# The three gate products of each recurrent block, moved one piece later on TensorE

## The chip, the cores and the metric

The kernel runs on one core of one Trainium2 chip. The metric is the device time of one launch in microseconds (us); lower is better. The five engines of the core run apart from each other and meet only in semaphores: TensorE (PE in the rows; its weight loads are PEld), VectorE (DVE), ScalarE (ACT), GpSimd (POOL) and SyncE (SP), which starts transfers.

## What is computed

One inference step of a hybrid decoder layer on 1024 prompt tokens and 8 sample tokens (1032 columns in all) with a model width of 1024. It has a recurrent branch (RG-LRU), a dilated attention branch, a merge of the two and a SwiGLU FFN. Only the recurrent branch matters here. Cut to its core:

```python
xn = rmsnorm(x, norm_mix)
lru_x, lru_g, q, k, v = split(xn @ w_in)
xc = causal_conv(lru_x, w_conv, b_conv)            # four taps
gate_a = einsum('btni,nij->btnj', xc, w_a) + b_a   # 16 blocks of 64 x 64
gate_x = einsum('btni,nij->btnj', xc, w_x) + b_x
r, i = sigmoid(gate_a), sigmoid(gate_x)
log_a = -8 * r * softplus(-lam)
a, mult = exp(log_a), sqrt(-expm1(2 * log_a))
u = mult * i * xc
h_t = a_t * h_{t-1} + u_t                          # a scan over the tokens
y_lru = (h * gelu(lru_g)) @ w_branch_lru
```

## The kernel before

The width is cut into eight blocks of 128 channels; channels lie on partitions, tokens along the free axis. A block of the recurrent stage needs two projections of the normed input, each called a **unit**: slot 0 gives the convolution's input `lru_x`, slot 1 gives `lru_g`. A unit is 72 matmuls (8 tiles of the contraction times 3 products of a split float32), in three **pieces** of 24, one for each third of the columns (344), and lands in its slot of the PSUM tile `ups`. The next stage, "qk", has units of the same size; its first one, qk(0, slot 0), follows the last recurrent block.

Between the pieces stand the **gate products**: `gates(i, c)` multiplies block i's convolved tile `XC` with the two 128 x 128 gate matrices in `bd`, for third c of the columns, into the two banks of `aux`. In a trace one call is four matmuls and four weight loads of line L754. All three calls of a block use the same two banks, so each waits in line L752 (`gate_ev`) until ScalarE has read the one before; the first also waits in L750 and L751 for the gate matrices and for the whole convolution (`xc_done`).

Here is one block on the other engines. The order is written out by hand and each engine keeps to it:

- VectorE: `side_in(i-1)` (L1571) takes slot 1 out of PSUM and frees it (`ps_free[1]`); `gated(i-1)` (L1578) multiplies the gate I with XC and waits for all three gates of block i-1; `branch_in(i)` (L1565) takes slot 0 out of PSUM; `conv(i)` (L1583, L1586) makes XC; `recur(i-1)` (L1594, L1595, L1599, the scan L1600, L1604) is the recurrence.
- ScalarE: `gate(i-1, 1)` (L1151, L1152: two sigmoids), GELU (L1158, behind `side_in`), `gate(i-1, 2)`, the transfers of the next gate matrices, `front(i)` (L1145, L1146), exp and tanh, the root L1169 in the midst of `recur(i-1)`, then `gate(i, 0)`. L1151 and L1158 need different function tables, each loaded in turn.
- GpSimd: `split` (L564, then L566) of the next weights, each time PE has finished a unit.

`front(i)` overwrites XC, so it waits for `gated(i-1)`; this ties one block of the recurrence to the next. In the qk stage PE's `stats` calls (L809) wait for GpSimd's low part of a square (L591, L596), which comes from a tile that VectorE takes out of PSUM at L1631. The first such tile comes before `recur(7)` in VectorE's order, the second after it.

Of the kernel before, what the change touches and what calls it, by code (L numbers as in the profile page):

```python
# [33 lines left out]
NCH = 3  # L34
CH = NT // NCH
KT = D // P
# [59 lines left out]
def build(nc, A, O):  # L96

    with ExitStack() as ctx:
        def sb(name, shape, dt=F32):
            return ctx.enter_context(nc.sbuf_tensor(name, shape, dt))  # L100
# [10 lines left out]
        big1 = sb("big1", [P, 2, KT, NT], F32R)  # L111
# [40 lines left out]
        def tmp(n):  # L152

            return x1[:, n, :]
# [557 lines left out]
        def _(pe):  # L712
            def unit(name, i, slot, src, nk=KT, parts=(0, 1, 2), ready=None, hi=0, held=None):

                if 0 in parts:
                    pe.wait_ge(w_split[slot], i + (T0[name] + 2))
                    if not held:
                        pe.wait_ge(ps_free[slot], i + (T0[name] + 1 - (12 if T0[name] >= T0["ylru"] else 0)))
                for c in parts:
                    if held:  # L720
                        held(c)
                    for k in range(nk):
                        if ready:
                            ready(c, k)
                        for n, (w, a) in enumerate(((0, hi), (0, 1 - hi), (1, hi))):
                            ins = nc.tensor.matmul(ups[:, slot, c, 0:CH], wsp[:, slot, w, k, :], src[:, a, k, c * CH:(c + 1) * CH],  # L726
                                                   start=(k == 0 and n == 0), stop=(k == nk - 1 and n == 2))
                if NCH - 1 in parts:
                    ins.then_inc(unit_done[slot], 1)
# [18 lines left out]
            def gates(i, c):  # L748
                if c == 0:
                    pe.wait_ge(bd_loaded, i * 64 + 64)  # L750
                    pe.wait_ge(xc_done, i + 1)  # L751
                pe.wait_ge(gate_ev, i * NCH + (c + 1))  # L752
                for a in range(2):
                    ins = nc.tensor.matmul(aux[:, a, 0:CH], bd[:, a, :], tmp(0)[:, c * CH:(c + 1) * CH], start=True, stop=True)  # L754
                ins.then_inc(gate_mm, 1)
# [18 lines left out]
            def lru(i):  # L774
                for c in range(NCH):
                    unit("lru", i, 0, big1, parts=(c,))
                    if c < 2:
                        gates(i - 1, c + 1)
                unit("lru", i, 1, big1)
                gates(i, 0)  # L780

            def first_evacuated(c):

# [2 lines left out]
            by_tiles("lru", big1, x_split)  # L786
            unit("lru", 0, 1, big1, parts=(0, 1))
            unit("lru", 0, 1, big1, parts=(2,), ready=norm_rows)
            unit("lru", 1, 0, big1, parts=(0, 1), held=first_evacuated)
            gates(0, 0)  # L790

            def second_gates(c, k):
                if k == 4:
                    gates(0, 1)

            unit("lru", 1, 0, big1, parts=(2,), held=first_evacuated, ready=second_gates)
            gates(0, 2)
            unit("lru", 1, 1, big1)
            gates(1, 0)
            with pe.Fori(2, KT) as i:  # L800
                lru(i)

            def stats(j, i, low=sq_parts[1]):

                pe.wait_ge(qsl_done[j], i + 1)
                pe.wait_ge(rt_done[1 - j], i + 1)
                for c in range(2):
                    for a, part_of in enumerate((sq_parts[0], low)):
                        ins = nc.tensor.matmul(aux[:, c, :], bones_r[:], part_of[:, c * 512:(c + 1) * 512], start=(a == 0), stop=(a == 1))  # L809
                ins.then_inc(st_done[j], 1)  # L810

            def qk(i, first):
                for j in range(2):
                    if first and j == 0:
                        for c in range(NCH):
                            unit("qk", i, j, big1, parts=(c,))
                            if c < 2:
                                gates(KT - 1, c + 1)
                    else:
                        unit("qk", i, j, big1)  # L820
                    if j:
                        if first:
                            pe.wait_ge(gate_ev, KT * NCH + 1)
                            stats(0, 0, first_low)
                        else:
                            stats(0, i)
                    elif not first:
                        stats(1, i - 1)

            pe.sem_inc(rt_done[1], 1)  # L830
            pe.sem_inc(st_done[1], 1)
            qk(0, True)
            with pe.Fori(1, 12) as i:
                qk(i, False)
# [25 lines left out]
            for g in range(NG):  # L860
                with pe.Fori(0, 4) as i:
# [20 lines left out]
                    for n in range(10):  # L882
# [19 lines left out]
                        if n >= 2:  # L902
# [4 lines left out]
                            for hh in range(2):  # L907
                                for k in range(nk):
                                    c = 256 * hh + 256 - P * (nk - k)
# [1236 lines left out]
```

## Time and profile before

| | us |
|---|---|
| median of three runs (lowest, highest) | 1946.58 (1945.2, 1947.05) |
| the profiled execution | 1945.86 |
| its span, first to last instruction | 1944.1 |
| mean granted TensorE clock | 0.998 of full speed |

The recurrent stage stands from about 40 to 245 us of the span, followed by the qk stage. The profiled execution is 0.72 us under the median and has 1.76 us around its span. Starts and durations in the rows are those of this execution.

### The profile page before, as it was taken

To read this page: it belongs to the slowest core of one execution; us is meant where nothing else is said; L and a number is where in the kernel's file an instruction comes from. 1 tells how busy PE (TensorE), PEld (TensorE's weight loads), DVE (VectorE), ACT (ScalarE), POOL (GpSimd) and SP (SyncE) were. 2 spreads that over 40 slices of the span, in tenths; PEclk is the share of its full clock that TensorE was granted. 3 is DMA by queue.
4 is the path that set the end of the run, shared out by engine and by line. 5 is a ranking of instruction groups with operands and counts; after the bars stand their busy time and mean duration, and the time that the engine had idled before them with its cause. 6 is when DMAs were issued, how large, how long until landed. Compare 5 with 4: busy or idle time off the path is not lost.

```text
span 1944.1 us, 34565 instructions
## 1 busy us (share of the span) xinstructions
PE 1918.2 (99%) x13148; PEld 1870.2 (96%) x13148; DVE 1145.4 (59%) x1373; ACT 616.8 (32%) x1035; POOL 873.3 (45%) x533
## 2 busy tenths in 40 slices
PE   7999999999999999999999999999999999999999
PEld 7899999999999999999999999999999999999999
DVE  5666688878844545444328663586554555455555
ACT  5655632222203333333320111333222232223222
POOL 3233254444434433534334332336655656455643
PEclk9999999999999999999999999999999999999999
DMA  6111112222254355544345652112111111211112
GB/s 244 43 46 35 45 70 86 86 86 86 87 171 131 128 158 173 171 160 149 128 161 182 209 194 87 65 33 66 50 39 50 61 55 34 65 45 61 34 59 110
DMA packets 85034, 191.73 MB, mean 99 GB/s; under 512 B 10445, under 2 KB 38600, under 8 KB 83408
## 3 DMA queue, kind: packets, MB, share of 16 engines
q1 hardware_dynamic: 57872, 142.92, 22.3%
q10 hardware_dynamic: 27072, 47.53, 7.1%
q8 instruction: 65, 1.06, 0.2%
q14 instruction: 25, 0.20, 0.0%
HBM read 147.81 MB, written 42.62 MB: 98 GB/s over the span
## 4 chain that ended last, share of the span: by engine, by line
PE 88%; DVE 5%; issue 2%; DMA 1%; ACT 1%; POOL 1%; ACTq 1%; SPq 0%; DVEq 0%; POOLq 0%
PE ups L726 30%; PE ups L870 14%; PE ups L995 13%; PE ups L1038 11%; PE aux L1038 8%; PE aux L910 3%; PE ups L889 2%; PE aux L900 1%; PE ups L767 1%; PE aux L809 1%; DVE x L1583 1%; DMA big_f<-x_R 1%; PE aux L754 1%; PE ups L900 1%; ACTq L1090 1%
## 5 line engine op out<-in xcount | busy, mean ns | idle before, releaser
L726 PE MATMUL ups<-big,wsp 128*128 128x344 f32 x4680 | 755.1, 321 | 0.7 <-issue 0.7
L726 PEld LDWEIGHTS ups<-big,wsp 128*128 128x128 f32 x4680 | 739.9, 188 | 8.8 <-issue 1.6
L564 POOL CAST wsp<-wraw 128x1024 fp32r<-128x1024 f32 (+1 forms) x96 | 104.6, 1089 | 658.0 <-issue 393.9
L674 POOL TENSOR_TENSOR wsp<-wraw,wsp 128x512 fp32r<-128x512 f32 x184 | 263.7, 1449 | 212.4 <-ACT wsp L1406 212.4
L870 PE MATMUL ups<-big,wsp 128*128 128x344 f32 x1728 | 302.6, 326 | 0.0
L870 PEld LDWEIGHTS ups<-big,wsp 128*128 128x128 f32 x1728 | 271.4, 189 | 3.5 <-issue 3.0
L995 PE MATMUL ups<-big,wsp 128*128 128x344 f32 x1584 | 254.4, 320 | 0.3 <-DVEq L1979 0.2
L995 PEld LDWEIGHTS ups<-big,wsp 128*128 128x128 f32 x1584 | 248.9, 188 | 3.9 <-issue 2.9
L1038 PE MATMUL ups<-big,wsp 128*128 128x258 f32 x1920 | 240.7, 283 | 1.4 <-ACT ext L1445 1.3
L1038 PEld LDWEIGHTS ups<-big,wsp 128*128 128x128 f32 x1920 | 234.9, 189 | 1.8 <-issue 1.8
L566 POOL TENSOR_TENSOR wsp<-wraw,wsp 128x1024 fp32r<-128x1024 f32 (+1 forms) x96 | 228.7, 2382 | 7.7
L1406 ACT ACTIVATE wsp<-wraw 128x512 fp32r<-128x512 f32 x184 | 113.2, 626 | 257.1 <-PE ups L995 128.7
L1038 PE MATMUL aux<-big,wsp 128*128 128x258 f32 x1440 | 181.5, 282 | 0.0
L1038 PEld LDWEIGHTS aux<-big,wsp 128*128 128x128 f32 x1440 | 175.9, 189 | 0.0
L2001 DVE TENSOR_TENSOR x<-ups,x 128x1032 f32<-128x1032 f32 x87 | 107.2, 1232 | 116.1 <-PE ups L995 116.1
L1645 DVE RECIPROCAL x<-x 128x1024 f32<-128x1024 f32 x24 | 157.2, 6551 | 5.0 <-ACT x L1222 4.9
L683 POOL TENSOR_TENSOR wraw<-wraw 128x512 f32<-128x512 f32 x80 | 112.3, 1404 | 71.1 <-DMA wraw<-w_ffn_in 63.1
L1785 DVE SCALAR_TENSOR_TENSOR x<-ups,ext 128x256 f32<-128x256 f32 (+1 forms) x96 | 52.0, 542 | 134.5 <-PE ups L889 133.8
L1222 ACT ACTIVATE x<-aux,epst 128x1024 f32<-128x1024 f32 x24 | 26.8, 1117 | 204.4 <-PE aux L809 194.1
L1302 ACT ACTIVATE x<-x 128x128 f32<-128x128 f32 (+1 forms) x192 | 75.5, 442 | 11.6 <-DVE x L1788 11.6
L910 PE MATMUL aux<-ext,x 128*128 128x65 f32 x560 | 73.1, 266 | 0.0
L1792 DVE COPY x<-aux 128x130 f32<-128x130 f32 x96 | 28.0, 292 | 74.6 <-PE aux L910 73.4
(248 smaller groups left out, 1870.5 us busy)
## 6 DMA issues: line engine op xcount, KB each, us to landing
wraw<-w_in SPq DMA_DIRECT2D x52, 512.0 KB, 3.9
wraw<-w_ffn_in SPq DMA_DIRECT2D x80, 256.0 KB, 2.6
x<-out_qkv SPq DMA_DIRECT2D x35, 512.0 KB, 4.2
out_qkv<-x ACTq DMA_DIRECT2D x32, 512.0 KB, 3.3
wraw<-w_ffn_out SPq DMA_DIRECT2D x44, 256.0 KB, 2.8
x<-gate_s SPq DMA_DIRECT2D x16, 516.0 KB, 4.6
wraw<-w_merge SPq DMA_DIRECT2D x16, 512.0 KB, 6.7
x<-o_s SPq DMA_DIRECT2D x8, 792.0 KB, 4.8
```

The costliest lines, as they stand in the source:

```text
L564: nc.gpsimd.tensor_copy(hi, raw).then_inc(w_hi, 1)
L566: nc.gpsimd.tensor_tensor(lo, raw, hi.bitcast(F32), ALU.subtract).then_inc(w_split[slot], 1)
L674: nc.gpsimd.tensor_tensor(lo, raw_at(b), hi.bitcast(F32), ALU.subtract).then_inc(f_lo, 1)
L683: nc.gpsimd.tensor_tensor(raw(to), raw(a), raw(b), op).then_inc(f_add, 1)
L726: ins = nc.tensor.matmul(ups[:, slot, c, 0:CH], wsp[:, slot, w, k, :], src[:, a, k, c * CH:(c + 1) * CH], start=(k == 0 and n == 0), stop= ...
L870: ins = nc.tensor.matmul(ups[:, 0, c, 0:CH], wsp[:, slot, w, k, :], big1[:, a2, k, c * CH:(c + 1) * CH], start=(k == 0 and w + a2 == 0), s ...
L910: ins = nc.tensor.matmul(o_bank[:, hh * (HD + 1):(hh + 1) * (HD + 1)], PTS[q % 2][:, c:c + P], VTOK[:, q + 1 - nk + k, hh, :], start=(k == ...
L995: ins = nc.tensor.matmul(ups[:, n % 2, c, 0:CH], w[:, n % 2 * 2 + k, :], part(hid_row(a, k), c), start=(k == 0 and m == 0), stop=(k == 1 a ...
L1038: ins = nc.tensor.matmul(bank[s], w[:, kk, :], sub(MOVING[n](a, kk), s), start=(first and kk == 0 and m == 0), stop=(kk == 3 and m == 2), ...
L1406: nc.scalar.activation(ring(b)[0], raw_at(b), ACT.Copy).then_inc(f_hi, 1)
L1645: step.step(nc.vector.reciprocal(rms_t, rms_t))
L2001: nc.vector.tensor_tensor(own, ups_v[n % 2], own, ALU.add).then_inc(d_ev, 1)
```

## The change

Each gate product stands one piece later on PE. In the loop, `gates(i, 0)` stood after the last piece of unit (i, slot 1), and `gates(i, 1)` and `gates(i, 2)` after the first and second piece of unit (i+1, slot 0). Now the three calls stand after the first, second and third piece of unit (i+1, slot 0). For block 0 they stand after the last piece of unit (1, slot 0) and the first two of (1, slot 1); for block 7 behind the three pieces of qk(0, slot 0). Nothing is added or taken away and no other engine's order changes.

```diff
             def lru(i):
                 for c in range(NCH):
                     unit("lru", i, 0, big1, parts=(c,))
-                    if c < 2:
-                        gates(i - 1, c + 1)
+                    gates(i - 1, c)
                 unit("lru", i, 1, big1)
-                gates(i, 0)
...
-            unit("lru", 1, 0, big1, parts=(0, 1), held=first_evacuated)
-            gates(0, 0)
-
-            def second_gates(c, k):
-                if k == 4:
-                    gates(0, 1)
-
-            unit("lru", 1, 0, big1, parts=(2,), held=first_evacuated, ready=second_gates)
-            gates(0, 2)
-            unit("lru", 1, 1, big1)
-            gates(1, 0)
+            unit("lru", 1, 0, big1, held=first_evacuated)
+            for c in range(NCH):
+                gates(0, c)
+                unit("lru", 1, 1, big1, parts=(c,))
...
-                            if c < 2:
-                                gates(KT - 1, c + 1)
+                            gates(KT - 1, c)
```

PE at the entry of the stage, from the second piece of unit (1, slot 0) to the head of the loop. The rows name the semaphores each instruction waits for:

```order
 L726 MATMUL ups<-big,wsp 128x344 x23
+L726 MATMUL ups<-big,wsp 128x344 [waits lx_done]
+L726 MATMUL ups<-big,wsp 128x344 x23
 L754 MATMUL aux<-x,bd 128x344 [waits gate_ev,xc_done,bd_loaded]
 L754 MATMUL aux<-x,bd 128x344
-L726 MATMUL ups<-big,wsp 128x344 [waits lx_done]
-L726 MATMUL ups<-big,wsp 128x344 x11
+L726 MATMUL ups<-big,wsp 128x344 [waits ps_free1,w_split1]
+L726 MATMUL ups<-big,wsp 128x344 x23
 L754 MATMUL aux<-x,bd 128x344 [waits gate_ev]
 L754 MATMUL aux<-x,bd 128x344
```

The first gate product of block 0 has moved from behind the second piece to behind the third, and the second one now has a whole piece of slot 1 ahead of it where it had half a piece of slot 0.

PE in the loop, from the third piece of unit (i, slot 0) to the loop's end:

```order
 L726 MATMUL ups<-big,wsp 128x344 x24
-L726 MATMUL ups<-big,wsp 128x344 [waits ps_free1,w_split1]
-L726 MATMUL ups<-big,wsp 128x344 x71
-L750 ISA
-L752 ISA [waits xc_done,bd_loaded]
+L752 REGISTER_ALU
 L754 MATMUL aux<-x,bd 128x344 [waits gate_ev]
 L754 MATMUL aux<-x,bd 128x344
-L800 REGISTER_ALU
-L800 COMPARE_AND_BRANCH
+L726 MATMUL ups<-big,wsp 128x344 [waits ps_free1,w_split1]
+L726 MATMUL ups<-big,wsp 128x344 x71
```

The 72 matmuls of slot 1 stood between the end of slot 0 and a gate product of the same block; now a gate product of block i-1, the third, stands ahead of them.

## Rows read from the trace of the kernel before

**Rows 1.** The page: busy time of each engine, share of the span, instructions.

```profile
PE 1918.2 (99%) x13148; PEld 1870.2 (96%) x13148; DVE 1145.4 (59%) x1373; ACT 616.8 (32%) x1035; POOL 873.3 (45%) x533
```

**Rows 2.** Waits on PE: who waited for whom, us in total, times, longest.

```profile
PE aux L754 <- ACT x L1152: 3.0, 3, 1.3
```

**Rows 3.** Timeline of PE: start, duration, line, tiles, [idle before and releaser].

```profile
50.05 1.39 PE L754 MATMUL aux<-x,bd 128*128 128x344 f32 x4 [0.42 <-issue]
...
53.89 1.42 PE L754 MATMUL aux<-x,bd 128*128 128x344 f32 x4 [0.56 <-ACT x L1152]
...
75.98 1.42 PE L754 MATMUL aux<-x,bd 128*128 128x344 f32 x4 [1.33 <-ACT x L1152]
76.98 4.20 PE L726 MATMUL ups<-big,wsp 128*128 128x344 f32 x24
...
134.17 15.53 PE L726 MATMUL ups<-big,wsp 128*128 128x344 f32 x96
149.53 1.32 PE L754 MATMUL aux<-x,bd 128*128 128x344 f32 x4
150.43 4.20 PE L726 MATMUL ups<-big,wsp 128*128 128x344 f32 x24
154.46 1.32 PE L754 MATMUL aux<-x,bd 128*128 128x344 f32 x4
...
208.03 1.42 PE L754 MATMUL aux<-x,bd 128*128 128x344 f32 x4 [1.15 <-ACT x L1152]
...
268.13 1.20 PE L809 MATMUL aux<-ext_r,bones_r 128*128 128x512 f32 x4 [0.27 <-POOL ext_r L596]
```

**Rows 4.** Timeline of DVE, same columns.

```profile
61.56 1.23 DVE L1578 TENSOR_TENSOR ext<-x 128x1032 f32<-128x1032 f32 x1 [3.08 <-ACT x L1152]
64.61 3.93 DVE L1583 SCALAR_TENSOR_TENSOR x<-ext,par,x 128x1024 f32<-128x1024 f32 x3 [1.82 <-ACT x L1146]
68.57 0.75 DVE L1586 SCALAR_TENSOR_TENSOR x<-stc,par,x 128x8 f32<-128x8 f32 x3
...
86.24 1.23 DVE L1565 TENSOR_TENSOR ext<-ups,ext 128x1032 f32<-128x1032 f32 x1
...
133.49 1.23 DVE L1571 TENSOR_TENSOR x<-ups,ext 128x1032 f32<-128x1032 f32 x1 [0.69 <-DVEq L1605]
138.14 1.24 DVE L1578 TENSOR_TENSOR ext<-x 128x1032 f32<-128x1032 f32 x1 [3.42 <-ACT x L1152]
139.29 1.23 DVE L1565 TENSOR_TENSOR ext<-ups,ext 128x1032 f32<-128x1032 f32 x1
...
151.63 3.17 DVE L1599 TENSOR_TENSOR x<-x,ext 128x1032 f32<-128x1032 f32 x1
...
245.26 1.23 DVE L1631 TENSOR_TENSOR x<-ups,ext 128x1032 f32<-128x1032 f32 x1
...
261.51 1.23 DVE L1631 TENSOR_TENSOR x<-ups,ext 128x1032 f32<-128x1032 f32 x1 [0.36 <-DVEq L1606]
```

**Rows 5.** Timeline of ACT, same columns.

```profile
51.56 1.28 ACT L1151 ACT_TABLE_LOAD   x1 [8.37 <-PE aux L754]
...
53.30 0.54 ACT L1152 ACTIVATE x<-aux,par 128x344 f32<-128x344 f32 x1
...
58.17 1.07 ACT L1158 ACTIVATE x<-x 128x1032 f32<-128x1032 f32 x1
...
150.36 1.07 ACT L1169 ACTIVATE x<-x 128x1032 f32<-128x1032 f32 x1 [2.85 <-DVE x L1595]
...
153.19 0.54 ACT L1152 ACTIVATE x<-aux,par 128x344 f32<-128x344 f32 x1
```

**Rows 6.** Timeline of POOL, same columns.

```profile
69.87 1.57 POOL L564 CAST wsp<-wraw 128x1024 fp32r<-128x1024 f32 x1 [8.97 <-issue]
...
149.86 1.38 POOL L564 CAST wsp<-wraw 128x1024 fp32r<-128x1024 f32 x1 [7.11 <-issue]
151.31 2.40 POOL L566 TENSOR_TENSOR wsp<-wraw,wsp 128x1024 fp32r<-128x1024 f32 x1
```

## The prediction

> **What bounds the kernel now.** First the page's busy times: PE is busy 99% of the span and every other engine 59% or less [rows 1]. The table of waits says that PE's gate products waited for ScalarE's sigmoids 3.0 us in three places [rows 2]. PE's timeline has the places: 0.56 us at 53.89, 1.33 at 75.98, 1.15 at 208.03, and 0.42 at 50.05, where block 0's convolution had just ended [rows 3]. That is 3.46 us, the most that moving these products can give back.
>
> Next, what PE needs for a block without waits. A gate call takes 0.90 us until the next matmul (149.53 to 150.43), a piece 4.03 us until the gate call behind it (150.43 to 154.46), and 96 matmuls 15.36 us (134.17 to 149.53) [rows 3]. A block is 3 x 0.90 + 2 x 4.03 + 15.36 = 26.12 us, before and after: the change has the same pieces and seams.
>
> Then the others, on which this case hangs. VectorE takes slot 0 of block 2 out of PSUM at 86.24 and the first qk tile at 245.26 [rows 4]: 159.02 us for six blocks, 26.50 each. That is more than PE's 26.12. VectorE and ScalarE form a **chain** that runs by itself: `side_in`, GELU, the third gate, `gated`, `branch_in`, `front`, `conv`, `recur`, and `side_in` again. It is less than 60% busy on each engine because they take turns, but it has no slack as a whole. In block 4 the third gate's sigmoids wait for GELU, and `gated` waits 3.42 us for them (138.14) [rows 4]; PE had written that product at 133.3. So PE is fed by the chain, and PE's waits at 75.98 and 208.03 are places where the chain has come too late.
>
> At the stage's end the chain decides too. The second qk tile leaves PSUM at 261.51, behind the last recurrence [rows 4], and PE's `stats` at 268.13 waits 0.27 us for what GpSimd makes of it [rows 3]. There is no slack there: what the chain loses by then, PE waits.
>
> **Term 1, the entry: +5.7 us.** Block 0's first product was reached at 49.63 (50.05 less 0.42) [rows 3]. It now has a piece ahead of it: 49.63 + 4.03 = 53.65. The second follows at 53.65 + 0.90 + 4.03 = 58.6, the third at 63.5. From the start of a product to the end of its sigmoids, with a table load between, it is 3.79 us (50.05 to 53.30 + 0.54) [rows 3, 5]. GELU's input is long there (GELU ran at 58.17) [rows 5]; it would run at 62.5, between the second and third gate, and be done before the third product is. So the third gate ends at 67.3 and `gated(0)` starts there, not at 61.56 [rows 4]: +5.7. Everything up to `branch_in(2)` hangs on it, since `front(1)` overwrites what `gated(0)` reads. PE does not need to wait yet: the sigmoids of the first product end at 57.4, ahead of 58.6.
>
> **Term 2, block 1: +0.6 us.** `conv(1)` starts 3.05 us after `gated(0)` (61.56 to 64.61) [rows 4], at 70.35. GpSimd's split starts when PE ends unit (1, slot 1), now about 68.5; before it was 69.87 [rows 6]. Two SBUF operands on VectorE and a GpSimd instruction exclude each other here: L1599 takes 3.17 us at 151.63, where GpSimd's subtraction runs until 153.71, and ends 1.09 us behind it [rows 4, 6]. Without a GpSimd instruction such a tile takes 1.23 (L1578) [rows 4]. The split holds 1.04 + 0.08 + 2.40 us, to 72.0, so `conv(1)` loses 1.65 us. It ended 7.76 us after `gated(0)` (68.57 + 0.75) [rows 4] and now ends at 67.3 + 7.76 + 1.65 = 76.7. PE reaches gates(1, 0) at 72.3: **a new wait of about 4.4 us**, longer than all the waits that go. The second product of block 1 then waits some 0.9 us more for its sigmoids, and the third stands at 87.6. Its sigmoids end at 91.4, and `branch_in(2)` follows 1.15 us behind `gated(1)`, as at 138.14 and 139.29 [rows 4]: 92.55 against 86.24. That is +6.3, of which 5.7 is term 1.
>
> **Term 3, six blocks: +1.2 us.** Now the third product stands behind slot 0's last piece, and the cycle runs through PE. Third product to the end of its sigmoids 3.79; to `gated` 0.03; to `branch_in` 1.15; from there to the root L1169 11.07 (139.29 to 150.36) [rows 4, 5]; to the end of the next block's first gate 3.37 (150.36 to 153.73) [rows 5]; to the second product 0.05; to the third 1.00 + 4.03 (the 1.00 from 75.98 to 76.98) [rows 3]. Sum 24.5 us. To this comes the collision with the split of slot 1. That split starts 12.7 us behind the third product (0.90 + 11.33 + 0.5) and holds the pair until 16.2 or later; L1594 and L1595 stand at 13.5 and 14.8, so they lose about 2.2 us; L1599, which lost 1.94 in the block at 151.63, then comes after it. 24.5 + 2.2 = 26.7 a block against 26.50 now: six blocks, +1.2. The ends: with no collision PE's 26.12 is the floor, 6 x (26.12 - 26.50) = -2.3; with GpSimd's copy in a convolution step and its subtraction in L1594 it is 1.2 us worse a block, +7. I take the middle since the starts put it there. With 26.7, PE waits some 0.5 us for L1152 at each second gate product, and slot 1 of PSUM is free 0.8 us before PE wants it.
>
> **Term 4, the exit: -0.4 us.** From 245.26 to 261.51 it is 16.25 us [rows 4], which holds several instructions that GpSimd held up. Placed again from 252.75, GpSimd's low part of the first tile, the last root and the split behind `stats` fall so that the second tile leaves at about 268.6: 15.85 us. It can be 2 us either way. PE itself would reach the second `stats` at about 272.7, with 1.5 us of new wait at the first one; the chain has it ready at 275.2. So PE waits 2.5 us more, and the stage is left at 275.2, not 268.13.
>
> **Sum.** 5.7 + 0.6 + 1.2 - 0.4 = **+7.1 us**. The qk stage behind it moves with PE as a whole. From the profiled execution's 1945.86 that is 1953.0; from the median, 0.72 us higher, **1953.7**. PE's four old waits are not a further term: PE no longer decides when the stage ends.
>
> The page "Perfetto Trace Analysis" of the Trainium skill, sections "Identifying the Most-Contended Engine" and "Optimization Strategy", says to take the engine with the highest occupancy, find the gaps between its slices and make what they depend on come sooner. By it the three waits on ScalarE are what the move is worth, and the sum would be a gain; what the chain of two half-busy engines costs would not be in it. It is the first rival.
>
> **Rivals.** (a) *Faster*: PE decides throughout, the four waits go and the chain's lag stays hidden. 1946.58 - 3.46 = **1943.1**. For it: the share of 99% [rows 1], and that each second product gets 4.9 us more time behind L1169. Against it: the wait at 268.13 shows no slack at the exit, and the 11.07 us from `branch_in` to the root [rows 4, 5]. It decides if the lag at block 1 is under the 3.8 us or so that the new place gives gates(1, 0); I get more than 7. (b) *The chain catches up*: no collision in the loop (-2.3 for +1.2) and an exit 2.5 us better than 16.25. 6.3 - 2.3 - 2.5 = +1.5: **1948.1**. For it: PE's floor is under the chain's 26.50, and the collisions depend on tenths of a microsecond. Against it: a split of 3.5 us comes twice a block, with VectorE at work two thirds of the time. (c) *Two collisions a block*: +7 for the +1.2 in term 3: +12.9, **1959.5**. For it: GpSimd's subtraction for slot 0 ends within 0.1 us of `gated`'s start, and the copy for slot 1 starts as the convolution ends. Against it: a hold at `gated` would last only its last tenths.
>
> **How the numbers follow.** Forecast 0.66, (a) 0.11, (b) 0.15, (c) 0.08. A measurement of this kernel can tell about 0.2%, 3.9 us, from no change. The forecast's own range goes from +4.5 to +9.5, by the exit's 2 us and the cycle: 1951 to 1956. The range takes in (b) and part of (c): 1948.0 to 1957.5. (a) falls just inside 0.2%, except where a little more is won: faster 0.04. Within 0.2%: the rest of (a), most of (b) and the low edge of the forecast, 0.23. Slower 0.73.
>
> **What would show it.** In the changed kernel's trace: `gated(0)` near 67.3; PE idle about 4.4 us before the gate product near 76.7, released by L1586; `branch_in(2)` near 92.5; loop blocks of about 26.7 us with L1595 or L1594 long and L1599 at 1.23; idle before the second `stats` of 2 to 3 us, released by L596. The forecast is wrong if PE reaches gates(1, 0) without a wait, if blocks fall to 26.12, or if the `stats` wait is gone.

## The result

| | us, median (lowest, highest) | profiled execution | span |
|---|---|---|---|
| before, 6 runs | 1946.8 (1945.13, 1947.13) | 1945.86 | 1944.1 |
| changed, 6 runs | 1957.94 (1956.94, 1963.18) | 1957.09 | 1955.2 |

The change makes the kernel slower: ratio 1.0064, 95% interval 1.0052 to 1.0076, about 11 us. The forecast was +7.1 us (1953.7) with a range up to 1957.5. The direction held; the forecast size was two thirds of what came, and the time lies just above the range.

PE's waits in the changed kernel (who waited for whom, us in total, times, longest):

```profile
PE aux L754 <- DVE x L1576: 4.7, 1, 4.7
PE aux L754 <- ACT x L1142: 3.1, 6, 0.7
...
PE aux L800 <- POOL ext_r L596: 2.2, 1, 2.2
```

Lines behind the edit have moved up by ten in the changed kernel: L1576 is the L1586 of before, L1142 is L1152, and so on; `stats` is L800 instead of L809. Where [rows 2] had 3.0 us, the gate products now wait 4.7 us in one place for the convolution, 0.5 to 0.7 us in each of six blocks for the sigmoids, and the second `stats` waits 2.2 us. The timeline of PE has the places (start, duration, [idle before]); they answer [rows 3]:

```profile
51.65 1.32 PE L754 MATMUL aux<-x,bd 128*128 128x344 f32 x4
...
75.03 2.36 PE L754 MATMUL aux<-x,bd 128*128 128x344 f32 x4 [4.65 <-DVE x L1576]
...
108.89 1.42 PE L754 MATMUL aux<-x,bd 128*128 128x344 f32 x4 [0.50 <-ACT x L1142]
...
277.70 1.20 PE L800 MATMUL aux<-ext_r,bones_r 128*128 128x512 f32 x4 [2.19 <-POOL ext_r L596]
```

And VectorE, to set beside [rows 4]: `gated(0)`, `conv(1)`, `branch_in(2)`, `conv(2)`'s short steps, two instructions of `recur`, and the two qk tiles.

```profile
65.26 1.24 DVE L1568 TENSOR_TENSOR ext<-x 128x1032 f32<-128x1032 f32 x1 [12.18 <-ACT x L1142]
68.31 5.68 DVE L1573 SCALAR_TENSOR_TENSOR x<-ext,par,x 128x1024 f32<-128x1024 f32 x3 [1.82 <-ACT x L1136]
...
91.50 1.23 DVE L1555 TENSOR_TENSOR ext<-ups,ext 128x1032 f32<-128x1032 f32 x1
...
99.12 3.84 DVE L1576 SCALAR_TENSOR_TENSOR x<-stc,par,x 128x8 f32<-128x8 f32 x3 [0.18 <-DVE x L1573]
...
104.21 1.23 DVE L1585 SCALAR_TENSOR_TENSOR x<-x 128x1032 f32<-128x1032 f32 x1
...
106.74 1.24 DVE L1589 TENSOR_TENSOR x<-x,ext 128x1032 f32<-128x1032 f32 x1
...
255.62 1.23 DVE L1621 TENSOR_TENSOR x<-ups,ext 128x1032 f32<-128x1032 f32 x1
...
271.06 1.23 DVE L1621 TENSOR_TENSOR x<-ups,ext 128x1032 f32<-128x1032 f32 x1 [0.36 <-DVEq L1596]
```

From 91.50 to 255.62 are six blocks in 164.12 us, 27.35 each; before they took 26.50. The short steps of the convolution, three of eight columns, take 3.84 us at 99.12, where three such steps took 0.75 at 68.57 in [rows 4] (0.97 in a block of the loop without a split on them, as shown below). L1589, the L1599 of before, is down from 3.17 to 1.24. GpSimd's split stands on the short steps:

```profile
99.43 1.04 POOL L564 CAST wsp<-wraw 128x1024 fp32r<-128x1024 f32 x1 [8.96 <-issue]
100.55 2.39 POOL L566 TENSOR_TENSOR wsp<-wraw,wsp 128x1024 fp32r<-128x1024 f32 x1
```

It does so in every block from 2 to 7 (3.84 to 3.89 us). That is where the prediction's third term went wrong. In the kernel before GpSimd paid a part of the collision (its copy took 1.38 us at 149.86 [rows 6]); here its copy takes 1.04 us, and VectorE pays all of it. So the two engines also hold each other up where no semaphore stands between them, unlike what the opening section says of the five engines.

### The profile page after: what moved, and what is told of

Read it like the earlier page. It is cut to its first block, busy times and chain, and to the rows that moved or that the text cites. A ratio compares the mean times of both kernels' runs of the same rounds, so it can differ in the third digit from the quotient of the medians.

```text
span 1955.2 us, 34565 instructions
## 1 busy us (share of the span) xinstructions
PE 1923.0 (98%) x13148; PEld 1871.1 (96%) x13148; DVE 1154.9 (59%) x1373; ACT 617.5 (32%) x1035; POOL 861.0 (44%) x533
## 4 chain that ended last, share of the span: by engine, by line
PE 87%; DVE 5%; issue 3%; ACT 1%; DMA 1%; POOL 1%; ACTq 1%; SPq 0%; DVEq 0%; POOLq 0%
PE ups L726 30%; PE ups L860 14%; PE ups L985 13%; PE ups L1028 11%; PE aux L1028 8%; PE aux L900 3%; PE ups L879 2%; DVE x L1573 1%; PE aux L754 1%; PE aux L890 1%; PE ups L767 1%; PE aux L800 1%; DMA big_f<-x_R 1%; PE ups L890 1%; ACTq L1080 1%
## 5 line engine op out<-in xcount | busy, mean ns | idle before, releaser
L564 POOL CAST wsp<-wraw 128x1024 fp32r<-128x1024 f32 (+1 forms) x96 | 99.9, 1041 | 672.7 <-issue 403.8
L674 POOL TENSOR_TENSOR wsp<-wraw,wsp 128x512 fp32r<-128x512 f32 x184 | 256.2, 1408 | 214.1 <-ACT wsp L1396 214.0
L1292 ACT ACTIVATE x<-x 128x128 f32<-128x128 f32 (+1 forms) x192 | 75.5, 443 | 10.9 <-DVE x L1778 10.9
```

The lines of the kernel that those rows point to most:

```text
L564: nc.gpsimd.tensor_copy(hi, raw).then_inc(w_hi, 1)
L674: nc.gpsimd.tensor_tensor(lo, raw_at(b), hi.bitcast(F32), ALU.subtract).then_inc(f_lo, 1)
```

## The experiments

The loss can be read off at two places of a trace: the mean block from `branch_in(2)` to the first qk tile, and the start of the second `stats`, where the stage is left. All runs are in one table. The kernel before was timed again on the chip of each group: 1947.14 us for the first four experiments, 1946.9 for the next four, 1946.59 for the last three. The traces do not enter the stage at the same time: PE goes on with its unit at 39.72 us in the trace of before, at 38.32 in the changed kernel's first one, and between 39.06 and 40.07 in the others. So differences of about 1 us between two rows of the last two time columns show nothing by themselves.

| kernel | median us | ratio to before (95%) | branch_in(2) | block, mean of six | second stats |
|---|---|---|---|---|---|
| before | | | 86.24 | 26.50 | 268.13 |
| changed | 1957.94 | 1.0064 (1.0052, 1.0076) | 91.50 | 27.35 | 277.70 |
| entry_only | 1953.74 | 1.0035 (1.0024, 1.0047) | 93.41 | 26.52 | 275.38 |
| loop_only | 1953.7 | 1.0038 (1.0023, 1.0053) | 88.02 | 27.35 | 274.13 |
| after_parked | 1950.1 | 1.0019 (1.0009, 1.0029) | 92.42 | 26.35 | 272.53 |
| exit_undone | 1961.1 | 1.008 (1.0062, 1.0098) | 93.24 | 27.47 | 282.37 |
| before_parked | 1947.2 | 1.0002 (0.9993, 1.0011) | 87.17 | 26.14 | 267.31 |
| loop_parked | 1943.41 | 0.9981 (0.9972, 0.9991) | 87.55 | 26.19 | 264.20 |
| after_swapped | 1960.48 (one run) | | 93.70 | 27.23 | 279.15 |
| after_again | 1958.83 | 1.0062 (1.0045, 1.0078) | 92.86 | 27.35 | 279.12 |
| before_parked_b | 1944.49 | 0.9986 (0.9978, 0.9995) | 85.60 | 26.14 | 265.74 |
| loop_parked_again | 1942.65 | 0.9979 (0.9968, 0.9991) | 88.39 | 26.19 | 265.04 |
| after_parked_b | 1946.16 | 0.9995 (0.9986, 1.0004) | 92.03 | 26.18 | 268.27 |

**The theory**: the chain of VectorE and ScalarE sets the stage, the change delays its start, and the new phase puts GpSimd's split on the chain in each block. **The rivals**: PE's own waits are the loss, or the third product's place behind slot 0 makes a block long whatever GpSimd does.

### Either half of the change alone

entry_only has the new entry, and the loop and the qk stage of before. Against the changed kernel's entry:

```diff
             for c in range(NCH):
                 gates(0, c)
                 unit("lru", 1, 1, big1, parts=(c,))
+            gates(1, 0)
```

> The kernel before with only the entry of the changed one: block 0's three gate products stand behind the last piece of unit (1, slot 0) and the first two of (1, slot 1); the loop and the qk stage are those of before. Chain theory (the lag of VectorE's and ScalarE's chain is what PE pays at the stage's exit): gated(0) starts about 5 us later, gates(1, 0) waits about 8 us for the convolution, blocks of 26.5 us as before, time +5 to +6.5 us over the kernel before, about 1952.5. Rival (the loss is made in the loop, the entry is hidden): within 2 us of the kernel before.

loop_only has the old entry without its last line, and the loop and the qk stage of the changed kernel. Against the entry of before:

```diff
             gates(0, 2)
             unit("lru", 1, 1, big1)
-            gates(1, 0)
```

> The changed kernel with the entry of before: block 0's gate products where they stood, block 1's and all later ones at the new places. Chain theory: branch_in(2) about 2 us later than before, no wait of 4.7 us, but the same phase between GpSimd's splits and the three small convolution steps L1586, so blocks of 27.3 us, +6 to +7 us over the kernel before, about 1953. Rival (the entry's lag is what makes the collision): blocks of 26.5 us or less, +2 us or less.

Both came out by the chain theory: +6.6 us for each by the medians, for entry_only just above the 5 to 6.5 that were expected. entry_only keeps blocks of 26.52 us and carries a lag of 7.2 us from `branch_in(2)` to the exit, unchanged (93.41 against 86.24, 275.38 against 268.13). Its new wait for the convolution (which ends at 76.08) is longer than in the full change, since gates(1, 0) is still at the old place:

```profile
76.18 2.63 PE L754 MATMUL aux<-x,bd 128*128 128x344 f32 x4 [8.22 <-issue]
```

loop_only is only 1.8 us late at `branch_in(2)` and has no such wait, but its blocks take 27.35 us. So the collision does not need the late entry: the loop's phase alone makes it. The two halves are not fully separate: they add up to 13.2 us, more than the 11 of the whole. The 1.8 us come from block 1's products at the new places, and the full change has them too.

### GpSimd's split taken off the chain

In after_parked the weights' split of slot 1 waits for the end of the running recurrence, from block 2 on:

```diff
+                if name == "lru":
+                    split(name, nk, 1, 0)
+                    split(name, nk, 1, 1)
+                    with pool.Fori(2, KT) as i:
+                        split(name, nk, i, 0)
+                        pool.wait_ge(z_done, i)
+                        split(name, nk, i, 1)
+                    continue
```

> The changed kernel, but from block 2 on GpSimd starts the split of slot 1's weights only when the running recurrence is over (it waits for z_done), so that it falls where VectorE waits or reads PSUM. Collision theory: the three small steps take about 1 us together again, blocks fall from 27.33 to PE's floor of 26.1 to 26.2 us, conv(1) takes 3.9 instead of 5.7 us, and the time is 8 to 9 us under the changed kernel, about 1949. Rival (the third gate product behind slot 0's last piece sets the block's length, whatever GpSimd does): blocks stay near 27.3 us and at most the 1.7 us of conv(1) is won, 1956 to 1958. A second risk: the split comes late for unit (i, slot 1), which would show as a PE wait for GpSimd's L566.

By the medians it is 3.0 us over the kernel before instead of 11.1: about 8 us are gone. In the trace the short steps are back at 0.97 us:

```profile
121.87 4.14 DVE L1581 SCALAR_TENSOR_TENSOR x<-ext,par,x 128x1024 f32<-128x1024 f32 x3 [2.02 <-ACT x L1144]
126.19 0.97 DVE L1584 SCALAR_TENSOR_TENSOR x<-stc,par,x 128x8 f32<-128x8 f32 x3 [0.18 <-DVE x L1581]
```

`branch_in` comes every 26.16 us there (118.63 to 223.26, four blocks); the mean of 26.35 in the table includes the last block, where the qk stage's split still collides. The parked splits now reach into `gated` (1.87 us at 116.84 instead of 1.23), but the block no longer hangs on it: it is at PE's 26.1. Nothing on PE was moved, so the rival that the product's place makes the block long falls. `conv(1)` is free of the split too, and PE waits 2.90 us for it instead of 4.65. That wait and the chain's lag at the exit (2.13 us before the second `stats`) are the waits that are left.

### Is it the short steps, or the hold?

after_swapped puts the three short steps of the convolution ahead of its long ones, so that the split meets long instructions:

```diff
                 dve.wait_ge(xc0_done, i + 1)
-                for k in range(1, 4):
-                    step.step(nc.vector.scalar_tensor_tensor(XC[:, 0:SEQ], LX[:, k:k + SEQ], par[:, ds(i, 1), k], XC[:, 0:SEQ], ALU.mult, ALU.add))
                 for k in range(3):
...
+                for k in range(1, 4):
+                    ins = nc.vector.scalar_tensor_tensor(XC[:, 0:SEQ], LX[:, k:k + SEQ], par[:, ds(i, 1), k], XC[:, 0:SEQ], ALU.mult, ALU.add)
+                    if k < 3:
+                        step.step(ins)
                 ins.then_inc(xc_done, 1)
```

> The changed kernel with the three 8-column steps of the convolution ahead of its three 1024-column ones, so that GpSimd's split of slot 1 meets a long step and L1584, L1585 instead of the short ones. If what counts is only how long GpSimd holds VectorE off (about 2.9 us wherever it falls), blocks stay at 27.2 to 27.4 us. If short instructions are what makes it dear, blocks fall to about 26.7 us, the figure of the prediction.

Blocks of 27.23 us, in one run. Now other instructions pay: the plain copy behind the convolution takes 1.01 us where it took 0.16 in the changed kernel, and L1585 3.29 us where it took 1.23.

```profile
129.28 1.01 DVE L1580 COPY sout<-ext 128x11 f32 x1
...
131.46 3.29 DVE L1585 SCALAR_TENSOR_TENSOR x<-x 128x1032 f32<-128x1032 f32 x1
```

The sum is about 2.9 us again. What counts here is how long GpSimd holds VectorE off while VectorE has work, not which instruction is met. The copy has only one SBUF operand, and yet it ended at 130.29, with GpSimd's copy (130.26). So in this trace the exclusion is not limited to instructions with two, as term 2 of the prediction had it.

### The exit

exit_undone is the changed kernel with block 7's products at the places of before:

```diff
                     if first and j == 0:
+                        gates(KT - 1, 0)
                         for c in range(NCH):
                             unit("qk", i, j, big1, parts=(c,))
-                            gates(KT - 1, c)
+                            if c < 2:
+                                gates(KT - 1, c + 1)
```

> The changed kernel with block 7's gate products at the places of before (one ahead of qk(0, slot 0), two behind its first two pieces). Chain theory: the third gate's sigmoids come behind GELU, which waits for side_in(7), so they can't be earlier than now; tile and exit stay, time within 1 us of the changed kernel, about 1958. Rival (each product's own place carries its 4 us to the end): 3 to 4 us under the changed kernel.

Neither: by the medians it is 3.2 us slower than the changed kernel. The old place is one piece too early for a chain that now lags; PE waits 3.74 us for `conv(7)`. The first qk tile comes 1.1 us later than in after_again (258.07 against 256.95), of which 0.3 us are older than block 7. Another 2.2 us are lost up to the second tile (275.75 against 272.40). PE's late unit starts GpSimd's split at 258.13, where after_again has it at 252.26, and the first two steps of `recur(7)`, 1.23 us each there, take 2.46 and 3.31.

```profile
241.33 2.63 PE L754 MATMUL aux<-x,bd 128*128 128x344 f32 x4 [3.74 <-issue]
```

```profile
262.78 3.31 DVE L1587 SCALAR_TENSOR_TENSOR x<-x 128x1032 f32<-128x1032 f32 x1
```

I had left this wait out: I asked only what the third product could gain, not what the first one would wait for. With a late chain the later place came out better, but the two intervals overlap (1.0052 to 1.0076 and 1.0062 to 1.0098), and 1.6 us of PE's delay at 241.33 is the half clock of the last section.

### The kernel before, and a faster one

If collisions cost the changed loop 2.9 us a block, they cost the old one too (1.94 at L1599, [rows 4]). before_parked is the kernel before with after_parked's edit; slot 0's split waits for `gated` as well, and the second and fourth split of the qk stage for the end of a recurrence. On top of that edit, the loop and then the qk stage:

```diff
+                        pool.wait_ge(u_done, i)
                         split(name, nk, i, 0)
...
+                    pool.wait_ge(z_done, KT)
                     split(name, nk, 0, 1)
                     split(name, nk, 1, 0)
                     first_square_low()
+                    pool.wait_ge(z_done, KT + 1)
                     split(name, nk, 1, 1)
```

> The kernel before with GpSimd's splits moved away from VectorE's instructions with two SBUF operands, from block 2 to the second qk tile: slot 0's split waits for gated, slot 1's for the end of the running recurrence. Theory (before the change too, collisions set the block, and the chain sets the exit): blocks fall from 26.50 to PE's floor of 26.12, the wait for L1152 near 208 us is gone, the last recurrence is 2 to 3 us shorter, so 3 to 4.5 us under the kernel before, about 1943. Rival (PE is at its floor anyway, 99% busy): within 1 us of it.

The blocks did as expected, 26.14 us, PE's floor, but the time did not move (about 1943 was expected). The wait for `gated` had put slot 0's split of block 2 on `conv(1)`:

```profile
64.50 5.78 DVE L1594 SCALAR_TENSOR_TENSOR x<-ext,par,x 128x1024 f32<-128x1024 f32 x3 [1.82 <-ACT x L1157]
```

It took 3.93 us there before [rows 4], and PE waited 1.59 us for it at gates(1, 0) and 0.69 at gates(1, 1). The 2.2 us won in the loop are PE's only in part: once blocks run at 26.12, PE sets the pace and every wait of its own counts.

loop_parked joins the old entry, the changed loop and qk places, and the waits for z_done alone, those of the qk stage included:

> The entry of before, the changed loop and qk places, and GpSimd's splits of slot 1 moved behind the recurrence, the two of the qk stage too. Theory: blocks at 26.1 to 26.2 us, branch_in(2) 1.8 us later than before as in loop_only, the exit 2 us shorter; 1.5 to 3.5 us under the kernel before, about 1944.5, and 8 us or more under loop_only. Rival (the new places cost by themselves): at or over 1950.

It beats both kernels: 1943.41 us, and unedited once more, beside the next kernel:

> loop_parked once more, unedited, beside before_parked_b on one chip: 1943 to 1944.5, at least 2 us under the kernel before.

1942.65 us, ratio 0.9979 (0.9968 to 0.9991). PE's products wait in two places only, 0.73 and 0.56 us at the entry. To see whether the changed loop has a share in this, before_parked_b has the same waits of GpSimd with the old loop:

> The kernel before with the same waits of GpSimd as loop_parked (slot 1's splits behind the recurrence, the two of the qk stage too; slot 0's free, unlike before_parked, where slot 0's met conv(1)). Theory: once the collisions are gone both orders of the loop run at PE's 26.1 us and what is left between them is the wait at gates(1, 1) near 76 us, 0.6 to 1.3 us: about 1944.5, no more than 1.5 us over loop_parked. Rival (the later places are worth something in the loop by themselves): 2.5 us or more over loop_parked.

1944.49 us. The medians differ by 1.8 us, but the intervals overlap, and at the second `stats` it is 0.7 us (265.74 against 265.04), about the wait of 0.62 us left at gates(1, 1). So both loops run at 26.1 to 26.2 us without collisions, and whether the new places are worth anything beyond that wait stays open; these runs can't tell.

after_parked_b is the full change with those waits:

> The changed kernel in full, its entry included, with the waits of loop_parked. Theory: what is left of the loss is the entry, PE's wait of 2.9 us for conv(1) and the chain's start 5 to 6 us late, part of which PE's floor of 26.1 takes up: exit 3 to 4 us later than in loop_parked, 1946.5 to 1948.5, 1.5 to 3 us under after_parked. Rival (the entry is hidden once the loop is free): within 1 us of loop_parked.

1946.16 us, no different from the kernel before. That is a little under the expected 1946.5 to 1948.5, and 3.9 us under after_parked where 1.5 to 3 were expected. Against loop_parked_again the stage is left 3.2 us later (268.27 against 265.04), as expected: that is the entry's own cost. PE waits 2.90 us at gates(1, 0), 0.48 at gates(1, 1) and 0.55 for GpSimd's split, which its new wait makes late; that is 3.9 us against 1.3 in loop_parked_again.

### The changed kernel again

> The changed kernel once more, unedited, for its spread between executions and for the 1.5 us that its first trace loses behind the qk stage. If these belong to the change, PE is again 1.5 us further behind the kernel before at the end than at 280 us; if they are the execution's own, the difference between these two places is another one. Time 1957 to 1959.

1958.83 us. Blocks are again 27.35 us. Its stage is left 1.4 us later than in the first trace (279.12 against 277.70), as it was entered: the first trace alone reached the entry 1.4 us sooner, as the last section shows. Behind the exit, the question was not settled by this run alone but by all of them: from 1392 us of the trace of before to the end, the same matmuls take 0.7 to 2.4 us longer in each of the twelve other traces, 1.4 in the first one of the changed kernel, 2.0 here, 1.4 and 2.1 in the two of the faster kernel. The kernels with the old order in the loop have it too (2.2 us in before_parked and in before_parked_b), so it does not come from the change. There is only one trace of the kernel before, and what made it quicker there is not shown.

## Why the prediction was wrong in size

**Terms 1 and 2, the entry: right in the mechanism, and near in size with some luck.** They gave +6.3 us at `branch_in(2)`. after_again, which entered the stage when the kernel before did, has 92.86 against 86.24: +6.6. `gated(0)` came at 66.63 (67.3 forecast), so term 1 was 5.1 us and not 5.7. `conv(1)` met the split as computed, 5.69 us instead of 3.93. The new wait was to be about 4.4 us before the product at 76.7, released by L1586; it was 4.66 us before 76.41, by that line. The next product was to wait 0.9 us for its sigmoids. It did not wait, since the half clock of the last section brought PE there 0.9 us after they had ended. Without that, an estimate from the same trace (sigmoids ended at 82.04, product at 83.04) puts `branch_in(2)` about 0.9 us sooner, at +5.7. So a lag that the prediction had no term for made good what term 1 had too much.

**Term 3, the loop: wrong by 3.9 us, and this is nearly the whole error.** It gave 26.7 us a block, +1.2 for six; it was 27.35, +5.1. The cycle without a collision was right: 24.5 us and a hold of 2.87 (3.84 less 0.97) make 27.37, against 27.35 measured. The step that failed is the hold, the time for which GpSimd keeps VectorE waiting in each block. I put the split from 12.7 to 16.2 us behind the third product, and that is where it stands (12.8 to 16.3 behind the product at 86.61). But I let it count only from L1594 on, at 13.5, and gave it 2.2 us. The three short steps stand in between, at 12.5, and have two SBUF operands as well. They waited for GpSimd like a long one and ended with its subtraction (102.96 and 102.94), so all that follows came 2.87 us late. Nor does the 2.2 follow from my own rows: an instruction that starts at 13.5 and ends 1.09 us behind the split, as L1599 did, would have ended at 17.3, 2.6 us late. So the hold was sized at 2.2 us instead of 2.9, and each missing tenth comes six times. after_swapped shows the hold to be about the same whichever instruction pays, after_parked that it sets the block. The upper bound, rival (c), is not consistent in the prediction: 1.2 us a block on top of the middle would be +8.4 us, and the +7 that was added up stands for blocks of 27.67 and a hold of 3.2. What happened, +5.1, lies between that and the middle, and I had given the middle 66%.

**Term 4, the exit: right within its 2 us.** From the first to the second qk tile it took 15.44 us; the forecast was 15.85 and before it was 16.25. The second `stats` waited 2.19 us (2 to 3 forecast), for L596. The new wait of 1.5 us at the first `stats` did not come: PE had no idle time there (263.10).

**The sum** with the measured terms is 6.6 + 5.1 - 0.8 = 10.9 us, and after_again leaves the stage 10.99 us late.

**The rivals.** (a), that the lag stays hidden, is refuted at all its points: PE waits 4.65 us where it should have had 3.8 us of slack. Its premise, that the busiest engine sets the pace, is also where the section "Identifying the Most-Contended Engine" of the Trainium skill's page "Perfetto Trace Analysis" leads. It names the engine with the highest occupancy, and judges TensorE's headroom by MFU (the share of its peak work that is done) and by the busy share of its weight loads. The traces do not agree with it here: PE is 99% busy before and 98% in the kernel that is 11 us slower, its weight loads 96% in both; no run here shows the MFU. (b), that the chain catches up, needed blocks at 26.12: they come only when the split is moved, as after_parked shows. (c) was right about the sign of the risk. The range ended 0.44 us too low because it took in only a part of (c), at 8%.

## What to carry to other kernels

When an engine is 99% busy, still measure the period of the chain that feeds it: if the chain's loop (26.50 us here) is as long as the bound engine's work (26.12), a piece of it moved later can delay everything. At the entry block 0's third product moved by 5.8 us (57.04 to 62.87) and the kernel lost 6.6 (entry_only). In the loop, the new places cost next to nothing once the splits were out of the way (26.19 us a block in loop_parked, 26.14 with the old places in before_parked_b). When a change shifts the phase between two engines, count every instruction under the collision, the eight-column ones too, and multiply by the number of rounds before choosing a middle value. Work without a near deadline, such as the splits here, can be released by the event after which its rival engine is idle: that alone was worth 8 us in the changed kernel, and with the old entry and the same waits in the qk stage it beat the kernel before by 0.2%.

## What the runs showed of the hardware that I had not expected

During or behind some of PE's waits the granted clock fell to half, from 2.4 to 1.2 GHz, for about 3.4 us, and in three traces for longer. In the changed kernel PE was idle for 4.65 us before 75.03; the stretches around it (stretch, length, PE busy, granted clock, DMA share, GB/s):

```profile
68.00:75.00 7.00, 2.38 (x16) 1.00 0.23 75
75.00:76.00 1.00, 0.97 (x2) 0.68 0.00 0
76.00:77.00 1.00, 1.00 (x4) 0.50 0.07 16
...
78.00:79.00 1.00, 1.00 (x5) 0.61 0.00 0
79.00:80.00 1.00, 1.00 (x9) 1.00 0.00 0
```

Four matmuls in a microsecond instead of nine. From the product at 75.03 to the next one PE took 6.65 us (to 81.68), where a product behind a wait and a piece take 1.00 + 4.03 us [rows 3]: 1.6 us on top of the wait itself. It was longer at this same product in exit_undone and after_swapped (6.8 us, waits of 4.65 and 4.69) and in entry_only (10.2 us, from 2.5 us after the start of its wait of 8.22); there the product and its piece took 2.1 to 2.3 us more than 5.03. It is not regular. In after_parked_b the wait of 2.90 us at this product had no such stretch behind it, in after_parked the wait of 2.90 us had one. All traces but the changed kernel's first one had such a stretch from about 36 us on, around PE's wait of 1.8 to 3.2 us for L741; there L741's 16 matmuls took 2.6 to 3.6 us, and 2.05 without it. This is the 1.4 us by which that trace came to the entry sooner. loop_only had it behind the wait of 2.14 us at its second `stats` (0.50 from 275 to 278), and so had after_parked (2.13) and after_swapped (2.23); the changed kernel's two traces did not behind waits of 2.19 and 2.28 us there. Behind one wait of 2.11 us near 583 us, in code that no kernel here touches, six of the thirteen traces had it, before and the changed kernel's first one among them; entry_only, loop_only, after_again and four more did not, which gave them 1.5 us back. In exit_undone it came on top of the wait of 3.74 us. So a new wait of a few microseconds on PE can cost PE 1.4 to 2.3 us more than its length, and single executions differ by 1.5 us; I had no term for it.
